# One layer step on one core: the first expert pair's tokens picked by matmul, and quarter loads at both ends of the expert stream

## The reference

```python
def hmoe(h, P, l):
    lg = xf @ w_router_group + b            # 4 groups; gi = argmax
    le = xf @ w_router_expert + b           # 4 x 8 experts; those of group gi are kept
    top_v, top_i = lax.top_k(le_g, 2)       # two experts per token
    wts = softmax(top_v) * p_grp
    # out = sum over the token's two experts of weight * (silu(h Wgate) * (h Wup)) Wdown
```

## Time and profile before

| | before |
|---|---|
| median of three runs | 1412.61 us |
| the profiled execution | 1410.4 us, span 1408.6 us |
| mean granted PE clock | 0.922 of full |
| PE, DVE busy in the span | 85%, 37% |
| DMA moved | 387.02 MB, mean 275 GB/s |

### The profile page before, as it was taken

One profiled execution on the slowest core, in us unless ns is written; L12 is line 12 of the kernel. 1 busy time (PEld: TensorE's weight loads), 2 busy tenths in 40 slices (PEclk: granted clock), 3 DMA queues, 4 the chain that ended last, 5 costly groups with the idle time before them and its releaser, 6 DMA issues.

```text
span 1408.6 us, 14842 instructions
## 1 busy us (share of the span) xinstructions
PE 1190.3 (85%) x5958; PEld 644.9 (46%) x5958; DVE 517.0 (37%) x989; ACT 195.8 (14%) x319; POOL 261.4 (19%) x568
## 2 busy tenths in 40 slices
PE   4789999998999899989989888778888888888740
PEld 2345555654556565656657553333333333333310
DVE  2412476565365464436552362111112121111208
ACT  1301110100120310232211140000000000000003
POOL 4071188885000000021120000000000000010010
PEclk9899999999999799889999979989999999999885
DMA  9999487865668367333123446999999999999944
GB/s 337 374 351 374 135 285 247 289 209 192 236 231 282 120 239 268 140 103 115 65 76 120 171 161 258 412 420 419 416 405 400 402 407 407 401 410 398 399 180 137
DMA packets 140102, 387.02 MB, mean 275 GB/s; under 512 B 15227, under 2 KB 54517, under 8 KB 112574
## 3 DMA queue, kind: packets, MB, share of 16 engines
q1 hardware_dynamic: 132208, 361.91, 68.3%
q0 software_dynamic: 6528, 18.72, 3.8%
q10 hardware_dynamic: 1296, 5.42, 1.1%
HBM read 385.95 MB, written 23.13 MB: 290 GB/s over the span
## 4 chain that ended last, share of the span: by engine, by line
PE 49%; DMA 26%; DVE 9%; POOL 9%; SPq 3%; issue 3%; ACT 2%; POOLq 0%; DVEq 0%; ACTq 0%
DMA slot<-in_w_exp_up 21%; PE psum L1109 11%; PE psum L1472 11%; PE psum L1397 5%; PE psum L1142 5%; DMA slot<-in_w_ada 3%; PE psum L1008 3%; PE psum L1038 3%; PE psum L1496 2%; POOL mem L559 1%; DMA mem<-in_w_exp_down 1%; POOL sq L557 1%; POOL sq L560 1%; POOL mem L562 1%; POOL sq L561 1%
## 5 line engine op out<-in xcount | busy, mean ns | idle before, releaser
L1472 PE MATMUL psum<-slot,mem 128*64 128x512 f32 x1024 | 254.6, 655 | 65.2 <-DMA slot<-in_w_exp_up 64.1
L1109 PE MATMUL psum<-hT,slot 128*128 128x320 f32 (+1 forms) x1056 | 297.7, 441 | 0.0
L1109 PEld LDWEIGHTS psum<-hT,slot 128*128 128x128 f32 (+1 forms) x1056 | 198.3, 190 | 96.5 <-issue 21.0
L1472 PEld LDWEIGHTS psum<-slot,mem 128*64 128x64 f32 x1024 | 81.0, 151 | 229.7 <-issue 153.7
L2216 DVE TENSOR_TENSOR sq<-sq,psum 128x256 f32<-128x256 f32 x16 | 6.7, 421 | 326.3 <-ACT sq L937 326.3
L1496 PE MATMUL psum<-mem,sq 128*64 128x512 f32 x512 | 115.0, 601 | 9.0 <-issue 7.1
L1008 PE MATMUL psum<-slot,cT 128*8 128x512 f32 (+1 forms) x768 | 103.5, 650 | 20.8 <-DMA slot<-in_w_ada 20.8
L629 POOL DMA_INDIRECT moe_output<-mem,idx x16 | 16.2, 1012 | 483.9 <-ACT mem L941 483.9
L1397 PE MATMUL psum<-mem,slot 128*128 128x320 f32 x256 | 70.8, 440 | 5.4 <-DVE mem L2031 5.4
L1496 PEld LDWEIGHTS psum<-mem,sq 128*64 128x64 f32 x512 | 42.1, 138 | 71.6 <-issue 70.1
L1142 PE MATMUL psum<-mem,slot 128*128 128x320 f32 x256 | 74.8, 448 | 0.0
(11 more groups left out here) (449 smaller groups left out, 1275.6 us busy)
## 6 DMA issues: line engine op xcount, KB each, us to landing
slot<-in_w_ada SPq DMA_DIRECT2D x48, 2048.0 KB, 10.2
slot<-in_w_exp_gate SPq DMA_DIRECT2D x64, 1024.0 KB, 12.6
slot<-in_w_exp_up SPq DMA_DIRECT2D x64, 1024.0 KB, 15.8
mem<-in_w_exp_down SPq DMA_DIRECT2D x32, 2048.0 KB, 16.6
slot<-in_w_in SPq DMA_DIRECT2D x17, 2048.0 KB, 11.7
slot<-in_w_out SPq DMA_DIRECT2D x8, 2048.0 KB, 8.0
mem<-in_w_in SPq DMA_DIRECT2D x2, 2048.0 KB, 18.0
mem<-in_x_prompt ACTq DMA_DIRECT2D x1, 2048.0 KB, 11.9
```

The lines of the kernel that those rows point to most:

```text
L1109: last = mm(psum[0:wd, grp % 2, 0:T], w[:, k, q * P:q * P + wd], hT[:, k, :], start=(k == 0), stop=(k == KD - 1))
L1472: last = mm(psum[rows_, 0, :].rearrange("p (w n) -> p w n", w=2), xe[i % 2][:, k, rows_], gate_up[h][:, :, k, :], start=(k == 0), stop=(k ...
```

## The change

Routing steps: the products over the four groups are written as one operation on a four-dimensional view instead of four, the sum over groups as one reduction instead of three additions; the softmax exponents and the copy of the ranks move behind the first result that PE needs.

Pair 0: its 128 slots are no longer gathered. DVE compares the ranks of experts 0 and 1 (the matrix `first_rank`) with the slot numbers, giving `first_at` (token by 128 slots, 0/1), and PE multiplies the rows `hn` with it (`select_x`): three matmuls, one per token tile, for each of the 16 blocks of 128 channels. `idle_work` and the gather of pair 0 are gone. Copies into `xe` wait only for the first token tile's store.

Table: the matmuls for `slot_rows` and for the overflow (`slot_table`) now stand inside `hidden(0)`, between k = 7 and k = 8; DVE's steps that make `slot_rows` of them, and POOL's gather of pair 1, follow from there.

Reversed slots: the odd expert of every pair now fills its slots from 63 downwards (`count_back`, `at_back`).

Quarters: the first half of pair 1's gate and up weights is loaded in two quarters, issued after k = 3 and k = 7 of `hidden(0)`; the second half of pair 15's in two quarters with a semaphore each; pair 15's down weights in column halves, the first for n = 0, 1 and the second for n = 2, 3.

```diff
+            both = [(h, w) for h in range(2) for w in range(2)]
             for i in range(1, NPAIR):
                 for q in range(2):
+                    if (i, q) == (1, 0):
+                        for quarter in range(2):
+                            sp.wait_ge(S("gu_used"), quarter + 1)
+                            for h, w in both:
+                                load_quarter(1, h, w, quarter, "gu_landed0")
+                    elif (i, q) == (NPAIR - 1, 1):
+                        sp.wait_ge(S("gu_used"), 2 * i + 1)
+                        for quarter, sem in ((2, "gu_landed1"), (3, "c_loaded")):
+                            for h, w in both:
+                                load_quarter(i, h, w, quarter, sem)
...
+            for half, sem in ((0, "dn_landed"), (1, "par_loaded")):
+                cols = slice(1024 * half, 1024 * half + 1024)
                 for h in range(2):
-                    load_dn(i, h)
+                    sp.dma_start(dn[h][:, :, cols], down[2 * NPAIR - 2 + h, :, :, cols]).then_inc(S(sem), 16)
...
-            pool.wait_ge(S("routed"), 3)
-            pool.wait_ge(S("h2_stored"), 48)
+            pool.wait_ge(S("routed"), 5)
+            pool.wait_ge(S("x_loaded"), 32 + 16)
+            pool.wait_ge(S("h2_stored"), 32)
...
-            for i in range(NPAIR):
-                if i >= 2:
+            for i in range(1, NPAIR):
+                if i >= 3:
...
+            def select_x(g_):
+                if g_ >= 2:
+                    pe.wait_ge(S("xe_ready"), g_ - 1)
+                for q in range(4):
+                    k = 4 * g_ + q
                     for j in range(3):
                         n = P if j < 2 else TS
+                        last = mm(bank(6 + g_ % 2, P, lo=q * P), hn[0:n, j, k * P:k * P + P],
+                                  first_at[0:n, j].rearrange("p h r -> p (h r)"), start=(j == 0), stop=(j == 2))
+                last.then_inc(S("xe_turned"), 1)
...
-                    if k % 8 == 7:
+                    if k % 8 == 7 or (i, k) == (0, 3):
                         last.then_inc(S("gu_used"), 1)
+                    if (i, k) == (0, 7):
+                        slot_table()
...
             pe.wait_ge(S("act_rows"), 12)
-            idle_work(4, 18)
+            pe.wait_ge(S("routed"), 2)
             for g_ in range(4):
-                turn_x(0, g_, 0)
-            pe.wait_ge(S("routed"), 6)
+                select_x(g_)
...
-            st(tt(ex4, G, bc(m3, [P, 3, 4]), SUB))
+            st(v.memset(oh4[64:P, 2, :], 0.0))
...
-            for g in range(4):
-                st(tt(le4[:, :, 8 * g:8 * g + 8], ...MUL))
-            st(tt(le, le4[:, :, 0:8], le4[:, :, 8:16], ADD))
-            st(tt(le, le, le4[:, :, 16:24], ADD))
-            st(tt(le, le, le4[:, :, 24:32], ADD))
+            st(tt(le4, lg[:, :, 4:36].rearrange("p j (g e) -> p j g e", g=4), oh4_wide, MUL))
+            st(v.tensor_reduce(le.unsqueeze(3), le4.rearrange("p j g e -> p j e g"), AX.X, ADD))
...
             dve.wait_ge(S("rank"), 1)
-            st(v.tensor_copy(rk[:, 0:2, :], bank(3, 64).rearrange("p (j e) -> p j e", j=2)))
-            st(v.tensor_copy(rk[0:64, 2, :], bank(3, NE, 64, lo=64)))
+            ranks = bank(3, 3 * NE).rearrange("p (j e) -> p j e", j=3)
+            st(stt(first_rank, ranks[:, :, 0:2], 1.0, Mk[:, :, 0:2], ADD, MUL))
+            st(tt(first_at, bc(first_rank.unsqueeze(3), [P, 3, 2, CAP]), bc(count_up.unsqueeze(1), [P, 3, 2, CAP]),
+                  ALU.is_equal), "routed")
```

More of the change, by code:

```diff
@@ L439, in _, with load_quarter @@
             down = a["w_exp_down"][0].rearrange("e (k p) n -> e p k n", p=P)
+            def load_quarter(i, h, w, q, sem):
+                part = slice(4 * CW * q, 4 * CW * (q + 1))
+                sp.dma_start(slot[:, 2 * h + w, part], (gate, up)[w][2 * i + h, :, part]).then_inc(S(sem), 16)
             def load_half(i, h, w, q):
@@ L933, in _ @@
             for i in range(NPAIR):
-                act.wait_ge(S("gu_used"), 2 * i + 2)
+                act.wait_ge(S("gu_used"), 2 * i + 3)
                 if i:
@@ L1432, in _, with slot_table @@
             for j in range(3):
-                n = P if j < 2 else TS
                 for jj in range(j + 1):
-                    last = mm(bank(3, NE, n, lo=NE * j), tri[:, 0:n] if jj == j else ones[:, 0:n], Mk[:, jj, :],
+                    last = mm(bank(3, NE, lo=NE * j), tri[:, :] if jj == j else ones[:, :], Mk[:, jj, :],
                               start=(jj == 0), stop=(jj == j))
             last.then_inc(S("rank"), 1)
-            pe.wait_ge(S("routed"), 2)
-            for h in range(2):
-                for c in range(2):
+            def slot_table():
+                pe.wait_ge(S("routed"), 4)
+                mm(bank(3, 3), ones[:, :], rt[:, 496:499], start=True, stop=True)
+                for h in range(2):
+                    for c in range(2):
+                        for j in range(3):
+                            n = P if j < 2 else TS
+                            last = mm(psum[CAP * h:CAP * h + CAP, 3, 128:160], (at_rank, at_back)[h][0:n, 3 * c + j, :],
+                                      tok_of[0:n, c, j, h].rearrange("p w i -> p (w i)"),
+                                      start=(c == 0 and j == 0), stop=(c == 1 and j == 2))
+                last.then_inc(S("rank"), 1)
@@ L1489, in expert_down @@
                 pe.wait_ge(S("actT_ready"), i + 1)
+                if i == 0:
+                    pe.wait_ge(S("routed"), 6)
                 for n in range(4):
+                    if n == 2 and i == NPAIR - 1:
+                        pe.wait_ge(S("par_loaded"), 16 * 17 + 32)
                     if i and n % 2 == 0:
@@ L2165, in _, with take_x @@
                 st(v.tensor_reduce(at[:, 3 * c:3 * c + 3].unsqueeze(2), am, AX.X, ADD))
-            st(tt(at_rank, bc(count_f.unsqueeze(1), [P, 6, CAP]), bc(at.unsqueeze(2), [P, 6, CAP]), ALU.is_equal), "routed")
             st(ts(over, at, float(CAP), None, ALU.is_ge))
             st(tt(rt[:, 496:499], over[:, 0:3], over[:, 3:6], ADD))
-            dve.wait_ge(S("rank"), 2)
-            found, row = psum[:, 3, 128:160], rt[:, 432:464]
-            st(ts(row, found, 0.0, float(NOWHERE + 1), ALU.is_equal, MUL))
-            st(tt(row, row, found, ADD))
-            st(ts(row, row, -1.0, None, ADD))
-            st(v.tensor_copy(slot_rows, row), "routed")
-            st(v.memset(rt[:, 471:472], 0.0), "routed")
+            st(tt(at_rank, bc(count_f.unsqueeze(1), [P, 6, CAP]), bc(at.unsqueeze(2), [P, 6, CAP]), ALU.is_equal), "routed")
+            st(tt(at_back, bc(count_back.unsqueeze(1), [P, 6, CAP]), bc(at.unsqueeze(2), [P, 6, CAP]), ALU.is_equal), "routed")
+            def take_x(i, g_, par):
+                dve.wait_ge(S("xe_turned"), 4 * i + (g_ + 1))
+                v.tensor_copy(xe[par][:, 4 * g_:4 * g_ + 4, :], bank(6 + g_ % 2).rearrange("p (k t) -> p k t", k=4))\
+                    .then_inc(S("xe_ready"), 1)
+            dve.wait_ge(S("x_loaded"), 32 + 16)
+            for g_ in range(4):
+                take_x(0, g_, 0)
             st(ts(keep, over, -1.0, 1.0, MUL, ADD))
```

79 lines of the change are left out of this document (41 added, 38 removed).

## The result

The changed kernel takes 1426.57 us (median of five runs, 1422.72 to 1432.77) against 1412.61 of the kernel before (five runs, 1408.89 to 1415.98): ratio 1.0090, 95% interval 1.0059 to 1.0121. It is 14 us slower; the forecast was 1411, and 1426.57 lies outside the range of 1404 to 1419. It is the time of the rival that had 6%: PE at half clock through `select_x`. The profiled execution took 1432.8 us, span 1430.9, mean granted clock 0.911.

The account below looks back on a forecast made before the run. The prediction took the unbroken weight stream, beginning at X, as the bound. X unchanged (0.0) and the end -0.8 gave 1409.6 us on the profiled execution, 1411.8 by the median; forecast 1411, range 1404 to 1419.

Parts of the forecast that it names:

- the rival that had 6%: PE stays at half clock through select_x: +14.6 us, less 0.8, giving 1426 us; chance 6%.
- What bounds it: Whole kernel: time is when the unbroken weight stream begins, plus its length, plus what follows its last landing.
- X: Issue of pair 1's down matrices on SP's queue, after expert_down(0): 876.88 before, forecast 876.9, unchanged.
- Routing: Steps ahead of select_x: fewer operations let it start at 830.5 instead of the table's matmuls at 834.14, gain 3.6 us.
- select_x: Pair 0's selection by 96 PE instructions at full clock: 14.6 us, low end 11.0, high end 29 at half clock.
- The Trainium skill's Part 4 on transposes: Transposes don't count as PE activity for the clock; select_x would then begin at half clock, adding 1.6 us.
- Table in hidden(0): 26 instructions inserted after the first half of hidden(0): 2.8 us, bounds 2.0 and 4.0.
- Gather of pair 1: Issued at about 858.0 in hidden(0), landing 6.4 us later; wait counted as 0.5 us, ends 0 and 8.
- expert_down(0): Pair 0's down contraction on PE, just ahead of X: kept at 8.70 us; the last pair's takes 7.09.
- From X to the end: Column halves of pair 15's down weights start the last expert_down earlier, -0.8 us; pair 15's quarters 0.
- The second rival: Gather of pair 1 lands late, PE waits up to 8 us at the turning: 1419 us; chance 18%.
- The first: Rival: pair 1's first load, 7 us earlier, counts in full; with the end -7.8, 1404 to 1405 us; chance 15%.

Follow-up runs that it names:

- e2: The changed kernel with the third token tile at its full 128 rows in the selection of x, so no height changes; 1408.69 us, ratio 0.9953.
- e9: The changed kernel with the selection's matmuls sorted by token tile in each group of four blocks, 8 height changes instead of 32; 1411.62 us, ratio 0.9974.
- e1: The changed kernel with ten idle matmuls on PE between the rank matmuls and the selection of x; 1412.92 us, ratio 0.9988.
- e4: The changed kernel with ten idle matmuls ahead of the selection of x and all 96 of its matmuls at full height; 1408.18 us, ratio 0.9951.
- e5: The kernel before with only the quarters and halves of the loads at both ends; 1410.96 us, ratio 0.9977.
- e6: e3 with pair 1's down matrices issued in column halves and two small routing steps put ahead of an overwriting; 1404.38 us, ratio 0.9925.
- e7: The changed kernel with idle matmuls, full height, the table after k = 3 of hidden(0) and pair 1's down matrices in column halves; 1407.31 us, ratio 0.9941.
- e3: The kernel before with the fewer routing steps and the quarters and halves of the loads at both ends; 1407.51 us, ratio 0.9949.

## Why the prediction was wrong, step by step

- *What bounds it* held: X and the stream behind it account for 13.2 of the 14.0 us.
- *Routing*: 3.5 gained for 3.6 forecast.
- ***select_x*, the step that failed.** "I count full clock; one short fall I put at 1.6." PE's idle time ahead, put at 1.2, was 1.74 and lay between the ranks and the selection; the clock fell in it and did not come back for 30 us: 30.0 for 14.6, +15.4. The high end of 29 was this case; I gave it 6% on the argument that the idle work had brought the clock back "with the same instructions". They were not the same: the idle work's instructions are all 128 by 128, and e2 and e9 show that the changes of height decide. The rows for it lay before me: 0.34 against 0.23 at a change of height is a break in the row, and I counted it as time only, not as something on which the clock could hang. (The 0.23 is twice the 0.115 of the earlier trace rows; in the earlier trace rows it stands only between pairs of 64 columns.) As time it was too small as well: 0.11 was put for each change, e1 shows 0.19 at full clock (16.9 in all). That the measured 1426.57 meets the 1426 of this rival so closely is in part luck: X came 1.8 later than its 14.6, and the stretch behind X shrank by 2.4 more than its 0.8.
- *The Trainium skill's Part 4 on transposes* (TensorE: Matmul & The Clock Gate), weighed there, would have had the selection start at half clock. It did, but as far as these runs show not for that reason: e1 has the same transposes, then ranks and idle matmuls without a wait, and stays at 1.00. And transposes alone brought the clock back in e2, where it had fallen ahead of them:

```profile
829.61 7.24 PE L1450 MATMUL psum<-ident,hT 128*128 128x128 f32 x48
```

```profile
829.60:832.00 2.40, 2.40 (x12) 2.40 (x12) 1.88 (x11) 0.99 (x2) 0.00 (x0) 0.50 0.00 0
832.00:833.00 1.00, 1.00 (x9) 1.00 (x8) 0.83 (x5) 0.74 (x2) 0.00 (x0) 0.73 0.00 0
833.00:836.00 3.00, 2.94 (x27) 2.47 (x26) 2.58 (x13) 2.57 (x6) 0.00 (x0) 1.00 0.53 218
```

PE did nothing but transposes from 829.61 to 836.7, and the clock went from 0.50 to 1.00 in the middle of them (in e4 and e5 as well). For these fp32 transposes the measurement differs from the page, and the measurement decides.
- *Table in hidden(0)*: 881.55 less 878.93 is 2.62, for 2.8.
- *Gather of pair 1*: PE waited for it, [3.08 <-DMA]; 6.4 us (888.64 to 895.04) instead of 4.8 passed to `expert_down(0)`, so 1.6 for the 0.5 put down. It was issued at 883.47 and landed after about 8 us, not 6.4; against the earlier trace rows:

```profile
883.47 1.12 POOL L663 DMA_INDIRECT mem<-moe_input,idx  x1 [146.34 <-DVE idx L2258]
```

```profile
DMA to landing us min/median/max: 8.2/11.5/11.8
```

- *expert_down(0)*: 7.09 for the 8.70 kept: -1.6. The low clock cost 1.5 in the first half of `hidden(0)` instead (8.63 for 7.09).
- *X*: by these terms 15.4 + 1.5 + 1.1 - 0.2 - 1.6 = +16.2, measured +16.4.
- *From X to the end*: -0.8 forecast, -3.2 measured; e5 alone has -2.5. The end gave 1.1 (hidden(15) to expert_down(15) 15.89 for 17.01). Of the rest I estimate that about 1 us is that X in the kernel before still had loads of pair 1 ahead of it (303 GB/s in the two microseconds after X, 74 after the change): I had those landing at "about 878", 1.1 behind X, and did not count that they would be out of the way. The last microsecond I can't place.

The second rival (the late gather) happened in small. The first (head start of 7 us in full) did not: DMA ran dry ahead of X in the changed kernel (119 GB/s from 900 to 902). e5, 3.3 us faster, rules out 7 us there too, but its head start is shorter.

## What to carry to other kernels

A short wait of PE is not only its own length: what follows it decides for how long the clock is lost. After a wait, a row with few or no changes of operand height got the clock back within 4 to 5 us (3.6 in e2, 4.2 in e9, 4.7 in the idle work of the kernel before); a row with two changes in every six instructions did not in 30. So sort matmuls by shape, or fill the rest with zeros, before counting them at full clock; and where a chain of transfers is bound by one release (X), try splitting the transfer at that release (in e6 and e7 it closed the dip; its worth in time is not shown).

## What was not expected of the hardware

- fp32 matmuls of 128 and of 64 rows in turn cost 0.19 us more for each change of height at full clock (e1 against e4: 6.0 us in 31). At half clock the weight load stands idle for 0.22 us at each (6.7 us in the 30 changes from 841 to 869).
- PE can count as busy without a stop, 10.00 of 10.00 us, and not get its clock back (850 to 860 after).
- Transposes alone can bring the clock back (0.50 to 1.00 between 832 and 833 in e2).
- Loads in quarters began more slowly: 227 to 285 GB/s in the first two full stretches of 2 us of pair 1's loads in e3 and e5, where the halves of the kernel before had 291 in their first full stretch of 2 us and then 418.
